# Hybrid conv and gated-linear-attention block: conv projections of the second half as seven products, their last three inside the next group

## The reference, cut to what matters

```python
u = rms_norm(h, g_pre)                    # h: 16 meta tokens + 2048 tokens, 1024 channels
proj = einsum('bld,dn->bln', u, w_in)     # c_b, c_c, c_x, c_z (1024 each), q, k (512), v, r (1024),
                                          # two low-rank gates (16), m_a, m_b (1024)
y_conv = c_b * short_conv_centred(c_c * c_x, conv_w) * silu(c_z)    # taps t-1, t, t+1
p_conv = y_conv @ w_out_c
y_gla  = rms_norm(gla_forward + gla_backward) * silu(r)             # chunked scans over q, k, v
p_gla  = y_gla @ w_out_g
out = (sigmoid(m_a) * p_conv + sigmoid(m_b) * p_gla) @ w_out
return h + rms_norm(out, g_post)
```

## Time and profile before

| | |
|---|---|
| runs of the kernel before | 2942.83 us median of 3 (2919.96 to 3392.01) |
| the profiled execution | 2921.19 us, span 2919.6 us on its slowest core |
| cores | 2909.6 to 2919.6 us, granted TensorE clock 0.995 to 0.997 |
| TensorE (PE) busy | 2851.8 us, 98% |
| DVE, ACT, GpSimd busy | 1815.4, 1381.3, 831.7 us |
| DMA | 373.44 MB |

### The profile page before, as it was taken

One profiled execution on the slowest core, in us unless ns is written; L12 is line 12 of the kernel. 1 busy time (PEld: TensorE's weight loads), 2 busy tenths in 40 slices (PEclk: granted clock), 3 DMA queues, 4 the chain that ended last, 5 costly groups with the idle time before them and its releaser, 6 DMA issues.

```text
span 2919.6 us, 53947 instructions; the slowest of 8 cores (2909.6 to 2919.6 us)
## 1 busy us (share of the span) xinstructions
PE 2851.8 (98%) x16092; PEld 1468.0 (50%) x16092; DVE 1815.4 (62%) x2786; ACT 1381.3 (47%) x2567; POOL 831.7 (28%) x1278
## 2 busy tenths in 40 slices
PE   6999999999999999999999999999999999999998
PEld 3565644444456554444456555444445655544443
DVE  4766662564677776465476677556457777745554
ACT  5766651232456764232256686323235767522222
POOL 3343333331323223232242312223123222321212
PEclk9999999999999999999999999999999999999999
DMA  7786548853633334374373323447356322354334
GB/s 183 134 140 116 125 101 183 232 173 113 197 106 77 75 84 115 110 232 127 111 216 81 75 68 89 123 142 230 97 152 170 78 72 71 84 137 127 118 112 140
DMA packets 340764, 373.44 MB, mean 128 GB/s; under 512 B 208112, under 2 KB 218352, under 8 KB 339968
## 3 DMA queue, kind: packets, MB, share of 16 engines
q1 hardware_dynamic: 326944, 344.61, 41.8%
q0 software_dynamic: 13536, 25.37, 6.0%
HBM read 287.69 MB, written 63.50 MB: 120 GB/s over the span
## 4 chain that ended last, share of the span: by engine, by line
PE 94%; DMA 2%; DVE 1%; issue 1%; POOL 1%; ACT 0%; SPq 0%; DVEq 0%; POOLq 0%; ACTq 0%
PE ps L479 94%; DMA sb_onT<-x 0%; DMA sb_onT<-sb_ON 0%; DMA wsc<-sb_W 0%; DMA sb_W<-w_all 0%; DMA sb_KT<-sb_GR 0%; POOL sb_stat L674 0%; PE ps L484 0%; POOL sb_SB L514 0%; DMA sb_ycT<-x 0%; DVE sb_CS L509 0%; DVE sb_ycT L505 0%; DVE sb_TB L509 0%; POOL sb_stat L514 0%; DVE sb_CS L505 0%
## 5 line engine op out<-in xcount | busy, mean ns | idle before, releaser
L479 PE MATMUL ps<-sb_uT,sb_W 128*128 128x512 bf16 (+2 forms) x7840 | 1625.9, 366 | 1.9 <-DMA sb_W<-w_all 1.2
L479 PEld LDWEIGHTS ps<-sb_uT,sb_W 128*128 128x128 bf16 (+1 forms) x7840 | 707.8, 98 | 808.9 <-issue 20.4
L496 ACT ACTIVATE sb_CS<-ps 128x512 f32<-128x512 f32 (+2 forms) x528 | 281.2, 540 | 636.2 <-PE ps L479 605.2
L505 DVE TENSOR_TENSOR sb_CS<-ps,sb_CS 128x512 f32<-128x512 f32 (+1 forms) x408 | 281.0, 691 | 187.9 <-PE ps L479 177.6
L509 DVE SCALAR_TENSOR_TENSOR sb_CS<-sb_CS,ps 128x512 f32<-128x512 f32 x256 | 175.8, 687 | 295.6 <-PE ps L479 284.3
L505 POOL TENSOR_TENSOR sb_GR<-sb_CS 128x512 bf16<-128x512 f32 x128 | 162.1, 1267 | 671.0 <-DVE sb_CS L509 658.5
L479 PE MATMUL ps<-sb_GR 128*128 128x512 bf16 (+2 forms) x1792 | 347.5, 318 | 1.1 <-POOL sb_GR L505 1.1
L505 POOL TENSOR_TENSOR sb_CS<-sb_CS 128x512 f32<-128x512 f32 x128 | 164.8, 1291 | 276.7 <-DVE sb_CS L509 168.6
L479 PE MATMUL ps<-sb_V,sb_uT 128*128 128x256 bf16 x2048 | 239.3, 274 | 0.0
L479 PE MATMUL ps<-sb_onT,sb_W 128*128 128x512 bf16 x1024 | 232.2, 379 | 2.6 <-DVE sb_onT L509 2.6
L509 DVE SCALAR_TENSOR_TENSOR sb_CS<-sb_CS,sb_convw 128x512 f32<-128x512 bf16 x256 | 209.8, 832 | 39.8 <-ACT sb_CS L496 27.6
(11 more groups left out here) (125 smaller groups left out, 2888.7 us busy)
## 6 DMA issues: line engine op xcount, KB each, us to landing
sb_W<-wsc SPq DMA_DIRECT2D x440, 256.0 KB, 2.6
sb_onT<-x SPq DMA_DIRECT2D x56, 512.0 KB, 5.4
sb_W<-wst SPq DMA_DIRECT2D x112, 256.0 KB, 2.8
sb_W<-w_all POOLq DMA_DIRECT2D x80, 256.0 KB, 6.2
sb_GR<-x SPq DMA_DIRECT2D x40, 512.0 KB, 5.5
wsc<-sb_W SPq DMA_DIRECT2D x80, 256.0 KB, 4.4
y<-sb_GR SPq DMA_DIRECT2D x32, 512.0 KB, 3.4
sb_ycT<-x SPq DMA_DIRECT2D x32, 512.0 KB, 5.4
```

What stands on the lines that cost most here:

```text
L479: S.add("pe", lambda e: e.matmul(out, lhsT=lhsT, rhs=rhs, start=start, stop=stop, skip_group_check=more), r, w, cost=max(0.025, free_n(rhs ...
L496: S.add("act", lambda e: e.activation(out=out, in_=in_, func=func, **kw), r, w, table=TABLE.get(func), cost=0.17 + 0.82e-3 * free_n(in_) + ...
L505: S.add(eng, lambda e: e.tensor_tensor(out=out, in0=a, in1=b, op=op), r, w, cost=ecost(eng, free_n(out), narrow(out, a, b)))
```

## The change

1. The conv blocks j = 2 to 7 of the second half go from `conv_units` to `conv7`: (cc, cx) and (z, cb) are each a group of seven products. In D2 a group's order is p1, p6, then p3, p7 of the group before, then p5, p2, then a stage 7 tile in two of three groups, then p4 of the group before.
2. The sums of weights for these 12 pairs are made once, in stage 6 of b = 0, hh = 0: `pair_sums` loads X and Y back from `wsc`, four DVE operations, two stores into `wst`.
3. `Seven` is rewritten: P1 is added in PSUM by DVE (p6), two partial results are copied out by ACT (p5); the order in stage 6 becomes p1, p6, p5, p2, oc 0, p3, p7, oc 1, og 1, p4, og 0.
4. First-half conv pieces become 342, 342 and 341 tokens (the last takes in the token to the right), and the one-column matmuls go, but for the meta token's in b = 0.
5. `W2` gets 8 buffers; regions SB, SM and ON are joined in `OS`, whose space holds partial sums in the second half; the DMA scratch falls to 4096.
6. At the start the first casts and the gate weights wait for norms of x tiles (`EARLY`), gbias comes later, and x tiles 8 to 15 wait for the square of tile i - 5.
7. The x tiles 2 to 7 of the next sequence are loaded during stage 6 of the second half. In the last stage 7, four x and y buffers in place of two; the residual is always added by DVE.

```diff
+        EARLY = {("k", 0): 0, ("q", 0): 1, ("lr", 0): 2, ("v", 0): 3, ("cc", 0): 5, ("cx", 0): 6, ("z", 0): 7, ("cb", 0): 8}
-                    [("SA", 0, {"W1": 1, "V": 2, "W2": 3}[self.name])] if n == 0 else after)
+                put("W" + self.name, lambda: self.load(n), None, [("SB", 0, EARLY[blk])] if first and blk in EARLY else after)
-        w2 = WPool("W2", [Buf("W2", i * 2048, 2048) for i in range(5)])
+        w2 = WPool("W2", [Buf("W2", i * 2048, 2048) for i in range(8)])
-            dma("sp", xv, x_d[0, i * 128:(i + 1) * 128, :], [], xk, ("xs", i), 1 << 19)
+            dma("sp", xv, x_d[0, i * 128:(i + 1) * 128, :], [], xk, ("xs", i), 1 << 19, [G["sq", i - 5]] if i >= 8 else ())
+        def pair_sums(pairs):
...
+            def load(n):
+                for z in range(2):
+                    ap, k = fetch[n % 2][z](BF16)
+                    dma("sp", ap, wsrc(wsc_d, pairs[n][1 + z]), [("wsc", pairs[n][1 + z])], k, ("wf", n % 2, z), 1 << 18)
...
+            for n in range(len(pairs)):
+                d = n // 2
+                put("SW", lambda n=n: load(n), None, [("qm", 0, 3, 1, 1), ("mb", 0, 0, d, n % 2)] + ([("SW", n - 2)] if n > 1 else []))
+                put("SX", lambda n=n: sums(n), ("SW", n), [("og", 0, 0, d, 1) if n % 2 == 0 else ("ma", 0, 0, d + 1, 1)])
...
+            def p5(self):
+                e = self.bank("e", True)
+                self.mul(e, 1, 0, self.tt(0), True)
+                self.keep(e, 2)
+                self.keep(self.bank("b"), 1)
+                rel(self.h[1])
+            def p6(self):
+                b_ = self.bank("b", True)
+                self.mul(b_, 1, 512, self.tt(1), True)
+                s_ap, s_k = self.sd[0](F32)
+                tt("dve", b_[0][:, 0:512], b_[0][:, 0:512], s_ap, ALU.add, b_[1] + s_k, b_[1])
...
+            cuts = [(0, 512), (512, 512)] if hh else [(0, 342), (342, 342), (684, 341)]
...
+            def total1(f, bk, part):
+                p_ = part(F32)
+                d = part(F32) if f else ccb(F32, 512, 512)
+                tt("dve", d[0], bk[0][:, 0:512], p_[0], ALU.add, bk[1] + p_[1], d[1])
+                if f == 1:
+                    times(pv(BF16, 513, 512), d, ccb(F32, 512, 512))
...
+            def tap(x):
+                t_ap, t_k = Buf("CS", 8704, 4096)(F32)
+                a_ap, a_k = pv(BF16, x, 1024)
...
+            g1 = Seven(8 + j, ("cc", j), ("cx", j), 1024, sdB, done1, total1)
+            g2 = Seven(16 + j, ("z", j), ("cb", j), 1024, sdC, done2, total2)
...
-                tsums(b, 1, [[("mb", 0, 0, 7, 1)]] * 4)
+                pair_sums(pairs)
+                tsums(b, 1, [[("mb", 0, 0, 7, 1), ("SW", len(pairs) - 1)]] * 4)
...
-                    a.append(("og", b - 1, 0, 7, 1))
+                    a.append(("mb", b - 1, 1, i - 2, 1) if 2 <= i < 8 else ("og", b - 1, 0, 7, 1))
...
+                for g in conv7(b, j):
+                    for p in ("p1", "p6"):
+                        put("D2", *g[p])
+                    if pend is not None:
+                        for p in ("p3", "p7"):
+                            put("D2", *pend[p])
+                    for p in ("p5", "p2"):
+                        put("D2", *g[p])
+                    if n % 3 < 2 and n and t7:
+                        put("D2", *t7.pop(0))
+                    if pend is not None:
+                        put("D2", *pend["p4"])
```

More of the change, by code:

```diff
@@ L446, in nps, with npk @@
                 G["held"] = G["held"] + (i,)
+            return psb[i], [("ps", i)]
+        def npk():
+            best = None
+            for i in range(8):
+                if i in G["held"]:
+                    continue
+                k = ("ps", i)
+                t = max([S.free["pe"]] + [S.last_w[k].end if k in S.last_w else 0.0] + [r.end for r in S.readers.get(k, ())])
+                t -= 0.0 if (i ^ 1) not in G["held"] else 0.4
+                if best is None or t < best[0]:
+                    best = (t, i)
+            if best is None:
+                raise NotReady()
+            i = best[1]
+            G["held"] = G["held"] + (i,)
             return psb[i], [("ps", i)]
@@ L629, in program @@
         e1 = Buf("AT", 4 * KB, 8 * KB)
-        ccb = [Buf("CS", i * 2048, 2048) for i in range(2)]
+        ccb = Buf("CC", 0, 4352)
         pvb = [Buf("CS", 4096 + i * 2304, 2304) for i in range(2)]
@@ L1587, in sa @@
                 G["s0", i] = sq_stat(*buf(i), *us(i))
+                G["sq", i] = S.ops["act"][-1]
             def sbf(i):
```

394 lines of the change are left out of this document (231 added, 163 removed).

## The result

The changed kernel takes 2978.18 and 2982.8 us in its undisturbed executions, the one before 2919.96 to 2942.83 beside it. Their ratio is 1.0188, with a 95% interval of 1.0136 to 1.0241, against a forecast of 2882.6 us. It is slower clear of noise; whether by more or less than 2% the interval leaves open. Some executions of either kernel run with one die at a lower granted clock and are left out of all comparisons here; two experiments (e4, e9) had only such executions, and there the cores of the other die are read.

The account below looks back on a forecast made before the run. PE's matmul time and idle time were taken to bound the kernel. From a span of 2919.6 us: -41.4 - 10.7 - 4 - 1.5 + 14 + 5 = 2881.0, plus 1.6 around it, 2882.6 us; range 2853 to 2922.

Parts of the forecast that it names:

- Seven products and the halo, as matmul time: PE's second-half conv groups and first-half pieces: fewer matmuls save 41.4 us, pieces without most one-column matmuls 10.7 us.
- DVE in the new conv stretch, +5: Second-half conv groups: DVE 80 to 88% busy, PE waiting twice the earlier 0.05 us a group, +5 us.
- Rival (b): Conv groups: some waiting in each for DVE or banks, 0.6 us a group, 29 us; 2907 us, chance 0.18.
- Rival (c): Conv blocks: cb's bank and DVE's long taps block the next group, 79 us; 2956.6 us or 2995, chance 0.07.
- Sums of weights, +14: b = 0's stage 6: extra DMA for the sums partly delays PE, +14 us, bounds -6 and +49.
- The estimate of +14 by the Trainium skill: b = 0's stage 6: at 358 GB/s a core, 16.2 us per d in place of 13.8, +14 us over six.
- Eight buffers of W2, -5 within that term: b = 0's stage 6: eight buffers in place of five let three casts go ahead, -5 us of DMA demand.
- 0 +- 3 for the new plan of phase 1: Phase 1: the planner's new order costs nothing, 0 with +-3 us.
- about equal work: First-half conv pieces: ACT and DVE get three shorter pieces for two and a halo, about equal work.
- a few us each: PE's waits before the change: the largest 23.3 us at the start, the others a few us each.
- The start, -4: Start: later first casts and gate weights let x tile 1 come some 5 us sooner, -4 us, bounds -6.5 and +3.
- The end, -1.5: Last stage 7 tiles: no wait for a store to free a buffer, stores one by one, -1.5 us, between 0 and -3.

Follow-up runs that it names:

- e4: Changed kernel with each group's p4 moved behind p1 and p6 of the group after the next; 3094.61 us for the whole program, with one die at a lower clock.
- e9: Changed kernel with b = 0's second-half conv blocks by eight products, sums made during them, og 0 before og 1; span 2956.5 us on core 5.
- e8: Changed kernel with the residual addition of stage 7's first half on GpSimd in place of DVE; 2971.77 us.
- e10: Changed kernel with p6 moved behind p3 and p7 of the group before, so three products lie between p7 and p4; 2943.97 us.
- e2: Changed kernel without the sums of weights for the conv groups, plain weight blocks of the same size loaded instead; 2951.8 us.
- e1: Changed kernel with second-half conv blocks by eight products again and no sums of weights for them; 2950.24 us.
- e6: e1 with five W2 buffers in place of eight; 2922.39 us.
- e5: Changed kernel with og 0 ahead of og 1 at the end of stage 6's order, as before the change; 2976.78 us.
- g2: f3 with the first casts issued behind the first x tiles, as before the change; ratio to the kernel before 0.9995.
- f3: f1 with first-half conv pieces of 512 tokens and one-column matmuls again; 2909.23 us median of seven, ratio to the kernel before 0.9973.
- g4: f3 run again unchanged on another chip; ratio to the kernel before 0.995.
- e7: e1 with first-half conv pieces of 512 tokens and one-column matmuls, as before the change; 2932.76 us.
- f1: e1 with five W2 buffers and og 0 before og 1 in stage 6; 2914.4 us.

## Why the prediction was wrong, step by step

- **Seven products and the halo, as matmul time.** Right: -51.4 where -52.1 stood. The width that the trace of before didn't have came out on the line: 1057.40 to 1059.73 is 2.33 us for 16, 145.6 ns each.

```profile
1057.40 2.49 PE L496 MATMUL ps<-sb_uT,sb_W 128*128 128x342 bf16 x16
1059.73 0.38 PE L496 MATMUL ps<-sb_GR,sb_CS 128*128 128x256 bf16 x2
```

- **DVE in the new conv stretch, +5.** The step that failed: +62, or 1.3 us a group. It took DVE's busy share (80 to 88% forecast, 60 to 63% measured over the conv groups) and twice the mean wait of the groups of stage 6, 0.05 us. Those have p4 as near behind p7, but beside a DVE without taps and tiles in its list; a mean over them says what the distance costs when nothing stands ahead of the total. In the conv groups something does, and p4 waits 33.4 us for it (0.70 a group); e8 took most of that away by shortening the list, e10 half by the order. Rival (b) had the kind of wait and half its price; against it stood that "p7 comes at least six products (5 us) after p6". That looked at one pair of products that share a bank and not at the next, p7 and p4, which the same order puts two apart. Rival (c) had about the size (79) by another way; e10 speaks against it, as the taps stayed and half the loss went.
- **Sums of weights, +14.** 27 to 28 (e2). A value near the lower bound was taken, as the load was spread over six values of d; with the queues at 94.7% of the time the excess didn't hide. The estimate of +14 by the Trainium skill, page "DMA: Bandwidth & Descriptors", section "Specifications" (358 GB/s a core), was as low. The trace has a mean of 253 GB/s here with the queues' time nearly used up, or 294 by an estimate that counts q0's 5.77 MB of bf16 as the fp32 that its casts read; so the mean stayed under that page's limit while the time of the queues ran out.
- **Eight buffers of W2, -5 within that term.** The wrong sign: between e1 and e6 they cost 13 us ahead of the first tile and 7 in phase 1 and stage 6. The term priced three casts that go ahead, and not that the planner orders all engines anew.
- **"0 +- 3 for the new plan of phase 1".** The ledger's +10.6 there. og's order takes 8 of it away (e5), five buffers 7 and pieces of 512 14; the last two were measured on e1, which loses 41.4 there, so the three don't add up to 10.6. The prediction counted for the pieces only their evacuations, "about equal work". It also read PE's waits as "a few us each" behind the start: the earlier trace rows leaves out the second largest, 9.9 us in 12 times for GpSimd's `sb_SB` in the scans, which is 13.3 in 16 times now (`sb_OS`).
- **The start, -4.** Right in kind, too small by itself (g2 against f3 and g4), and in the changed kernel given back before 400 us, where the three pieces lose 12 us more (e1 against e7).
- **The end, -1.5.** From the last matmul to the end it is -4.4, by 12.9 and 8.5 us; no run takes this edit alone.

Of the span, -38.6 us were forecast and +53.8 came on core 3, a miss of 92.4: 57.0 in the conv stretches (62.0 for 5), 25.9 ahead of the first tile (35.9 for 14 - 4), 10.6 in phase 1 and stage 6, 0.7 in the matmuls, 1.0 in the last tiles, and -2.9 at the end. The 25.9 are about the sums' other half (13) and the eight buffers (13); the start's 12 to 16 (g2 against g4 and f3) and the pieces' 12 to 16 (e1 against e7, f1 against f3) about cancel there.

## What to carry to other kernels

Where a matmul goes on adding to a bank that another engine must first read, hold the time of the matmuls between the two against all that this engine may have queued in front of its reading. Neither the engine's busy share nor the distance alone says it: 8 matmuls between p7 and p4 cost 0.09 us a group in stage 6 and 0.70 in the conv groups, and one product moved was worth 36 us here. When work is taken off the late engine, look in the trace at which wait it was that went, and not only at the time: e8 took 25 us of p4's waits away and gave nearly all of it back elsewhere. A saving in matmul count is bought with waits at both ends of the new schedule: price the distance of every pair of products that share a bank, and the place of the preparation. More buffers are not a gift where a planner orders everything by them; a kernel with more of them is another plan, and has to be measured as one.
